# Two of twenty Strassen pieces as plain products, attention's values one item later, and earlier low parts before the first down product

## What is computed

```
# first block
x   = layer_norm(x)
o_a = rms_heads(fox_attention(q_a, k_a, v_a, logf))          # 8 heads of 64, causal, 4 query tiles each
o_r = rms_heads(hgrn2(q_r, k_r, i_r, logf_r)) * silu(g_r)    # recurrent heads
x   = layer_norm(alpha * x + concat(o_a, o_r) @ w_o)
h   = depthwise_conv(x @ w_up);  a, u = split(h)
x   = layer_norm(alpha * x + (gelu(a) * u) @ w_down)
# second block
x   = x + g1 * merge(neighbourhood_attention(...), hyena(...)) @ w_out
h2  = modulate(rmsnorm(x), sh2, sc2)
x   = x + g2 * (silu(h2 @ w1) * (h2 @ w3)) @ w2              # up: w1 and w3, down: w2
out = rmsnorm(x)
```

## Time and profile before

| | |
|---|---|
| three runs, us | 1707.61, 1707.92, 1709.17 (median 1707.92) |
| profiled execution, us | 1708.51 |
| its span, first to last instruction | 1706.7 |
| mean granted TensorE clock | 0.976 |
| busy: PE, DVE, ACT, POOL | 1595.5, 1056.9, 700.4, 439.5 us |

### The profile page before, as it was taken

How to read it: one execution, slowest core, us unless ns; L and a number is a source line. 1 busy time by engine, 2 the same in 40 slices (tenths; PEclk the granted TensorE clock), 3 DMA queues, 4 the chain that set the end, 5 groups by cost and what they waited for, 6 DMA issues and landing times. The chain is left out here.

```text
span 1706.7 us, 21205 instructions
## 1 busy us (share of the span) xinstructions
PE 1595.5 (93%) x8576; PEld 1335.1 (78%) x8576; DVE 1056.9 (62%) x1458; ACT 700.4 (41%) x1021; POOL 439.5 (26%) x360
## 2 busy tenths in 40 slices
PE   5999988988999999999799999998899899998996
PEld 5778875766878888788788778887787899998885
DVE  6675547447987486433765543346853699998333
ACT  5644245543533243323632334444444544443222
POOL 0023303320622011100052012223432655553002
PEclk8999999989999899999899999999999999999998
DMA  7242212342254254222426423224443132224211
GB/s 285 99 148 75 75 62 89 118 176 99 99 173 164 107 197 173 99 99 74 147 99 248 130 76 109 85 84 152 151 166 124 38 112 99 99 100 148 76 73 50
DMA packets 46924, 203.93 MB, mean 119 GB/s; under 512 B 14337, under 2 KB 14721, under 8 KB 28203
## 3 DMA queue, kind: packets, MB, share of 16 engines
q1 hardware_dynamic: 37202, 171.84, 28.1%
q0 software_dynamic: 9088, 30.38, 5.3%
q10 hardware_dynamic: 536, 0.35, 0.1%
HBM read 181.56 MB, written 21.00 MB: 119 GB/s over the span
## 5 line engine op out<-in xcount | busy, mean ns | idle before, releaser
L540 PE MATMUL ps<-xh,whi 128*128 128x512 f32 (+1 forms) x1096 | 395.5, 361 | 10.8 <-DVE wlo L1742 5.3
L542 PE MATMUL ps<-xh,wlo 128*128 128x512 f32 (+1 forms) x1096 | 390.0, 356 | 0.0
L541 PE MATMUL ps<-xl,whi 128*128 128x512 f32 (+1 forms) x1096 | 388.2, 354 | 0.0
L1742 DVE TENSOR_TENSOR wlo<-raw,whi 128x2048 fp32r<-128x2048 f32 x93 | 233.3, 2509 | 138.3 <-ACT whi L1132 138.3
L1132 ACT ACTIVATE whi<-raw 128x2048 fp32r<-128x2048 f32 (+1 forms) x173 | 221.9, 1310 | 137.8 <-PE ps L542 52.1
L540 PEld LDWEIGHTS ps<-xh,whi 128*128 128x128 f32 x1096 | 208.8, 190 | 53.0 <-issue 11.6
L541 PEld LDWEIGHTS ps<-xl,whi 128*128 128x128 f32 x1096 | 209.2, 191 | 29.3
L542 PEld LDWEIGHTS ps<-xh,wlo 128*128 128x128 f32 x1096 | 207.9, 190 | 31.0
L540 PE MATMUL ps<-whi,xh 128*128 128x512 f32 x304 | 122.9, 404 | 8.3 <-ACT vr L1132 3.7
L542 PE MATMUL ps<-whi,xl 128*128 128x512 f32 x304 | 121.8, 401 | 0.0
L541 PE MATMUL ps<-wlo,xh 128*128 128x512 f32 x304 | 121.6, 400 | 0.0
(11 more groups left out here) (449 smaller groups left out, 3358.2 us busy)
## 6 DMA issues: line engine op xcount, KB each, us to landing
raw<-in_w_in SPq DMA_DIRECT2D x35, 1024.0 KB, 5.1
raw<-in_ffn_w SPq DMA_DIRECT2D x33, 1024.0 KB, 4.8
raw<-in_ada SPq DMA_DIRECT2D x24, 1024.0 KB, 4.8
raw<-in_w_up SPq DMA_DIRECT2D x22, 1024.0 KB, 4.8
raw<-in_w_down SPq DMA_DIRECT2D x11, 1024.0 KB, 4.8
xd<-X POOLq DMA_DIRECT2D x8, 512.0 KB, 6.1
td<-vr POOLq DMA_DIRECT2D x16, 256.0 KB, 3.6
raw<-td SPq DMA_DIRECT2D x4, 1024.0 KB, 5.3
```

The lines of the kernel that those rows point to most:

```text
L540: pe.e.matmul(o, lh, rh, start=start, stop=False)
L541: pe.e.matmul(o, lh, rl, start=False, stop=False)
L542: return pe.e.matmul(o, ll, rh, start=False, stop=stop)
L1742: up(ve.e.tensor_tensor(lo, raw[conv_at[j] % 3][:, :], hi.bitcast(F32), ALU.subtract), "wlo")
```

## The change

**Attention.** The loop runs to 36; `gather` and DVE's `scaled` lag four items instead of three. The recurrent mixes come at items 11 to 14 instead of 9 to 12. After the loop `mix` 5 and 6 come ahead of the head norm 3, on DVE and on ACT; `last_mixed(3)` comes within the first group of rows of `w_o`, after two of its four tiles.

**First down product.** High and low parts of pieces 0, 1 and 2 are made at (j2, part) = (10, 1), ahead of the last two up tiles; `pieces` begins with 3.

**Last up product.** Pieces 0 and 19 (`SLOW`) are made by eight products (`whole_tile`: two tiles of 48 matmuls, each with two quarters of weights), with four low parts, no sums of weights and no sums of results. Weights have eight slots instead of ten, ACT leads by seven, DVE by six. The token sum of product 7 is kept in place (`xs7`), two strips of 128 columns a row. The first four buffers of the down operand move to ones that are free after n = 18, and J_DOWN2 is made high after n = 18 is done.

The diff, cut to its core:

```diff
+SLOW = (0, 19)
+FAST = [(n, p) for n in range(N_FAST) for p in ((11, 21, 12, 22) if n in SLOW else (1, 2, 5, 6, 3, 7, 4))]
...
+def slot(q):
+
+    return (q - len(FAST)) % 8
...
-        dn2 = [(flat(xh4[i // 2][0])[:, 512 * (i % 2):512 * (i % 2) + 512], flat(xl4[i // 2][0])[:, 512 * (i % 2):512 * (i % 2) + 512])
-               for i in range(4)]
+        dn2 = [(x[:, 0:512], x[:, 512:1024]) for x in (flat(s2h), flat(s2l), xrf[:, 3, :], flat(cl)[:, 1024:2048])]
...
-                    if 9 <= i <= 12:
-                        pe.wait_ge(sig["rec"], i - 8)
-                        mix_turn(i - 9, tiles_of(orr, i - 9))
+                    if 11 <= i <= 14:
+                        pe.wait_ge(sig["rec"], i - 10)
+                        mix_turn(i - 11, tiles_of(orr, i - 11))
...
-                if i >= 3:
-                    hd, t = divmod(i - 3, 4)
-                    gather(i - 3, pt1[(i - 3) % 3], [va[:, q, P * (hd // 2):P * (hd // 2) + P] for q in range(t + 1)])
+                if i >= 4:
+                    hd, t = divmod(i - 4, 4)
+                    gather(i - 4, pt1[(i - 4) % 3], [va[:, q, P * (hd // 2):P * (hd // 2) + P] for q in range(t + 1)])
...
-                    between=lambda: last_mixed(3))
+                    after=lambda n: None if n else last_mixed(3))
...
+            def whole_tile(n, m):
+
+                p1, p2 = ((11, 21), (12, 22))[m]
+                b = take(("fast", n, p2), *(("f_a", FA["gated" if m else "gated21", n]) if n % 2 else
+                                            ("f_s", FS[f"silu{p2}", n])))
+                pe.wait_ge(sig["wlo"], item_no(n, p2))
+                for c in range(2):
+                    for k in range(8):
+                        h, l = place(FAST_AT[n, p2 if k // 4 else p1])
+                        o = mm3(b[:, 256 * c:256 * c + 256], h[:, k % 4, :], l[:, k % 4, :], half_tokens(xh4, k, c),
+                                half_tokens(xl4, k, c), k == 0, k == 7)
+                done(o, ("fast", n, p2))
+                fills.at["fast", n, p1] = fills.n
...
             head_squares(7, oa, 3)
+            mix_high(5)
+            mix_high(6)
             spectrum(14)
             head_roots(ms_f[:, 24:32], 64, 8)
-            mix_high(5)
             spectrum(15)
-            mix_high(6)
             high(J_WO + 1)
...
+                    if (j2, part) == (10, 1):
+
+                        ac.wait_ge(sig["ch_lo"], 20)
+                        ac.wait_ge(sig["act"], 3)
+                        for k in range(3):
+                            act(dn1[k][0][:, :], act1[:, k, :], ACT.Copy, "sp_hi")
...
-                if q + 9 < len(FAST):
-                    fast_high(q + 9)
+                if q + 7 < len(FAST):
+                    fast_high(q + 7)
...
             for m in range(2):
                 b = tile(("u2", 0, 1, m))
                 ve.wait_ge(sig["f_s"], m + 1)
                 up(ve.e.tensor_tensor(act2[:, m, :], b[:, :], yg[:, 512 * m:512 * m + 512], ALU.mult), "f_a")
-            rows_sum(3, 7)
-            for q in range(5, 8):
+            for q in range(2, 6):
                 fast_low(q)
...
-                if q + 8 < len(FAST):
-                    fast_low(q + 8)
-                if q == 136:
+                if q + 6 < len(FAST):
+                    fast_low(q + 6)
+                if (n, p) == (N_FAST - 1, 21):
                     conv[0] = J_DOWN2
                     low_parts(J_DOWN2)
-                if q == 138:
-                    pieces(1, act2, dn2, only=range(4))
+                    for k in range(4):
+                        low_part(dn2[k][1], act2[:, k, :], dn2[k][0], "down1", k)
```

More of the change, by code:

```diff
@@ L212, with last_of, before @@
 for _n, _p in FAST:
-    for _x in (["s1"] if _p == 2 else []) + (["silu"] if _p == 1 and _n % 2 else []):
+    for _x in (["s1"] if _p == 2 else []) + (["silu"] if _p in (1, 11) and _n % 2 and _n - 1 not in SLOW else []) \
+            + ([f"silu{_p}"] if _p in (21, 22) and _n % 2 == 0 else []):
         FS[_x, _n] = len(FS) + 3
-    for _x in {5: ["c11"], 6: ["u2"], 7: ["u34", "c22"], 4: ["c"] + ["gated"] * (_n % 2)}.get(_p, []):
+    for _x in {5: ["c11"], 6: ["u2"], 7: ["u34", "c22"], 4: ["c"] + ["gated"] * (_n % 2),
+               21: ["gated21"] * (_n % 2), 22: ["gated"] * (_n % 2)}.get(_p, []):
         FA[_x, _n] = len(FA) + 3
-TS = {x: 17 + i for i, x in enumerate((n, p) for n in range(N_FAST) for p in (5, 7, 6, 4))}
+TS = {x: 17 + i for i, x in enumerate((n, p) for n in range(N_FAST) if n not in SLOW for p in (5, 7, 6, 4))}
+def slot(q):
+    return (q - len(FAST)) % 8
+def last_of(n):
+    return 22 if n in SLOW else 4
+def before(n):
+    while n - 1 in SLOW:
+        n -= 1
+    return n - 1
 def item_no(n, p):
@@ L463, in place @@
         def place(q):
[L465 to L472, removed]
+            s = slot(q)
+            b = buffer_of(J_DOWN2) if s < 4 else buffer_of(J_UP2 + 1)
+            c = 512 * (s % 4)
+            h, l = whi[b][:, c:c + 512], wlo[b][:, c:c + 512]
             return tuple(x.rearrange("p (k c) -> p k c", k=4) for x in (h, l))
@@ L805, in tensor_program @@
             use[0] = "attention"
-            for i in range(35):
+            for i in range(36):
                 if i < 32:
@@ L1423, in scalar_program, with pieces @@
                         channels(u)
-            def pieces(inst, src, dn, ready, first, begun=0, only=None):
+            def pieces(inst, src, dn, ready, first, begun=0):
                 def one(k):
@@ L1438, in one @@
                     act(dn[k % 4][0][:, :], src[:, k, :], ACT.Copy, "sp_hi")
-                for k in only or range(begun, 4):
+                for k in range(begun, 4):
                     one(k)
-                for k in range(0 if only else NFF):
+                for k in range(NFF):
                     if k % 2 == 0:
@@ L1683, in scalar_program @@
             fast_high(1)
+            ac.wait_ge(sig["ch_lo"], 37)
+            act(xs7[0], xs_src[7], ACT.Copy, "ch_hi")
             ac.wait_ge(sig["pe"], at["w", J_UP2])
@@ L1687, in scalar_program @@
                 b = tile(("u2", 0, 0, m))
-                ac.wait_ge(sig["ch_lo"], 39)
+                ac.wait_ge(sig["ch_lo"], 40)
                 act(yg[:, 512 * m:512 * m + 512], b[:, :], ACT.Silu, "f_s")
[L1690 to L1694, removed]
+            for q in range(2, 7):
                 fast_high(q)
             for q, (n, p) in enumerate(FAST):
-                if p == 1 and n % 2:
+                if p in (21, 22) and n % 2 == 0:
+                    b = tile(("fast", n, p))
+                    ac.wait_ge(sig["f_a"], FA["gated", n - 1] if n else 2)
+                    act(yg[:, 512 * (p - 21):512 * (p - 21) + 512], b[:, :], ACT.Silu, "f_s")
+                elif p in (1, 11) and n % 2 and n - 1 not in SLOW:
                     ac.wait_ge(sig["f_a"], FA["c", n - 1])
@@ L2155, in vector_program @@
                         ada_sums((12, 21).index(2 * j2 + part))
+                    if (j2, part) == (10, 1):
+                        for k in range(3):
+                            low_part(dn1[k][1][:, :], act1[:, k, :], dn1[k][0][:, :], "down0", k)
                     for m in range(2):
@@ L2167, in vector_program, with pieces @@
                         channels(u)
-            def pieces(inst, src, dn, begun=0, only=None):
+            def pieces(inst, src, dn, begun=0):
                 def one(k):
                     low_part(dn[k % 4][1][:, :], src[:, k, :], dn[k % 4][0][:, :], f"down{inst}", k)
-                for k in only or range(begun, 4):
+                for k in range(begun, 4):
                     one(k)
-                for k in range(0 if only else NFF):
+                for k in range(NFF):
                     if k % 2 == 0:
@@ L2439, in vector_program @@
             fast_low(1)
-            rows_sum(2, 3)
-            for q in range(2, 5):
-                fast_low(q)
+            ve.wait_ge(sig["ch_hi"], 39)
+            up(ve.e.tensor_tensor(xs7[1], xs_src[7], xs7[0].bitcast(F32), ALU.subtract), "ch_lo")
+            rows_sum(3, 3)
             for m in range(2):
```

110 lines of the change are left out of this document (60 added, 50 removed).

## The result

The changed kernel takes 1684.87 us (median of four, 1683.75 to 1690.43) against 1708.55 for the kernel before on the same chip: ratio 0.9865, 95% interval 0.984 to 0.9891, 23 us faster. The forecast was 1688.6 with a range of 1681 to 1700. The profiled run has a span of 1682.1 where before has 1706.7.

What follows compares the result with a forecast made beforehand. TensorE's work (93% of the span) plus its stops and half clock were taken as the bound. Gains of 6.6 (attention), 3.2 (first down product) and 9.5 (last up stage), 19.3 in all, took 1707.92 to 1688.6 us, range 1681 to 1700.

Steps and rivals of the forecast that it cites:

- Part A: Attention through the output product: fewer stops and less half clock, 6.6 us gained, bounds 2 and 12.
- Iterations 9 to 14: Attention loop: the 3.00 us stop on `pt`, half clock and smaller stops shrink; 4.0 us gained of at most 5.7.
- Iterations 30 to 35: End of the attention loop: two stops before `gather` and their half clock shrink; 2.0 us gained, 0.5 to 3.5 possible.
- Output product: Attention's end: `wo` starts 2.7 us earlier, `rows_last` only 2.3, less 1.7 of half clock; 0.6 us gained.
- Part B: First down product: early low parts let it start without its stop; 3.2 us gained, bounds 0 and 3.4.
- Part C: Last up stage: earlier start, fewer steady stops, earlier down product without half clock; 9.5 us gained, bounds 5 and 12.
- if DVE's cycle stays: Last up stage, steady part: DVE keeps 21.25 us a pair of pieces, so 4.8 us of 7.1 of stops remain.
- The first: Attention gives little, 0 to 2 us, as DVE or ACT bounds it and loads land late; 1694.2 us, chance 0.18.
- The second: Longer unbroken stretches of PE bring one more half-clock stretch without a stop; 1693.7 us, chance 0.10.
- The third: Last up stage: the shorter lead no longer hides late sums or copies, gain only 4 us; 1694.1 us, chance 0.12.
- the fourth: Last up stage: DVE's and PE's waits lock, pairs exceed 21.25 us; at 24.0 a pair 1710.6 us, chance 0.05.
- The fifth: Last up stage: first and last pieces keep their stops, no gain there, attention gives 1; 1703.7 us, chance 0.05.

Runs made afterwards that it cites:

- e1: The kernel before with the attention part of the change alone; ratio 0.9968, 5.5 us faster.
- e3: The kernel before with the last up product's part of the change alone; ratio 0.9911, 15.2 us faster.
- e4: The kernel before, ten slots and seven products in every piece kept, with ACT's lead cut from nine to seven and DVE's from eight to six; 0.9926, 12.7 us faster.
- e6: The changed kernel with DVE's lead seven instead of six; ratio to the kernel before 0.9906, 16.1 us faster than that.
- e5: The kernel before with DVE's lead seven instead of eight, ACT's left at nine; ratio 0.9967, 5.6 us faster.
- e9: The changed kernel unchanged, timed again on another chip as its measure; 1686.56 us, ratio to the kernel before 0.9876.

## Why the prediction was right, point by point

**Sum and sign.** 19.3 forecast, 23.1 measured (24.6 between the profiled runs). The sign, the places and the order of the parts were right; each part is told below.

**Part A, 6.6 forecast, 5.5 measured in e1.** The size came out right in part by luck: the terms didn't come as they were reasoned. Distances between the same matmuls of before and after give them. *Iterations 9 to 14, 4.0 forecast:* 3.5 from the matmul at 253.18 (252.06 in after) to item 20. The 3.00 us on `pt` went, as forecast. That nothing takes their place failed: the mix stands behind DVE's low part of `Xr` still, and that one takes 5.24 us now (it took 2.92 in the earlier trace rows). It ends 2.15 us behind GpSimd's second sum of the spectrum (288.67 to 289.96), and that of before ends 2.16 behind this one:

```profile
293.75 1.26 POOL L2508 TENSOR_TENSOR spo<-spe,spo 128x512 f32<-128x512 f32 x1
```

So of the 4.7 us that stop and clock could give, 0.5 came, and the half clock behind is as long as it was (3.4). The other 3.0 came from four shorter stops between 266 and 285, 3.75 together, which are one of 0.77 now and which the forecast had at about 1. *Iterations 30 to 35, 2.0 forecast:* 2.6 from item 20 to the end of PE's work ahead of `wo`. Its two stops stayed (1.28 and 2.24, were 1.60 and 1.70); one half-clock stretch less (1.7) and smaller waits made it. *Output product, 0.6 forecast:* 1.8 lost, the term of A that had the wrong sign. The step "wo starts with a stop of 1.2" failed: the stop is 4.46, on the PSUM bank that ACT's copy of spectrum 15 frees, with ACT's table load and root ahead of it. The clock there is 0.52 for 6.8 us, where the forecast had 1.00. I had followed that copy only to POOL and its loads, not to the bank. The step "row loads late, affine from 386.9" failed too: the loads are issued at 367.64 to 369.3 and land within 10.6 us, so by 380, and the affine operations start at 382.25 right behind the low part of 380.04, which hangs on ACT and that on PE's first half. So what was won ahead passed through, 5.9 us of it by 392.77, the stop there grew from 2.22 to 3.53, and half clock behind it took 1.7, as forecast. So 6.1 were won ahead of `wo`, where the forecast had 6.0 by other stops, and the output product gave some of it back instead of adding to it.

**Part B, 3.2 forecast, 3.3 in the traces.** Right in its steps: three low parts of 0.62 at 685.48, the convolution behind them not seen by PE, down without a gap.

**Part C, 9.5 forecast, 14.4 in the traces, 15.2 in e3.** Start: 2.1 forecast; n=1 starts at 1352.26 where it was 1364.79, less the 10.2 won before, 2.3. End: half clock behind the down start gone, 1.6. The term that was mis-sized is the steady part: "if DVE's cycle stays" 21.25, 4.8 us of stops remain. The cycle went to 20.15 and no stop remains: 4.8 us, the whole of the difference 14.4 − 9.5. So the sign "gates 21.25 apart" failed. I took DVE's 20.65 us in 21.20 as a load that the change can't touch; a third of it was contention: low parts cost 15.7 us a pair, 9.4 with GpSimd out of the way, 10.7 after. The lead of eight to six, which I priced as 2.9 us of lost slack, was, with ACT's from nine to seven, the main gain (e4: 12.7 of 15.2 us). That the gain of C was forecast at all rests on the start and the end; the steady part came larger than reasoned, and through a mechanism that the forecast doesn't have.

**Rivals.** The first (attention gives little) did not come: 5.5. The second, one more half-clock stretch without a stop, neither; the one at 572.8 is there again, and it is no evidence for that rival (see the last section). The third and the fourth were wrong in sign: the shorter lead made the pairs shorter. Pairs longer than 21.25 came only in e6, with one product of lead more than the change has, by slow low parts and DVE's waits for ACT. The fifth fell with e3.

## To carry to other kernels

When two elementwise engines work beside each other, an engine's busy share isn't a fixed load: look at the duration of one form of instruction alone and beside the other engine before taking its cycle as a bound. The distance of a software pipeline decides what lies beside what, so try it one up and one down; here one number was worth 5.6 us (e5), with ACT's lead beside it 12.7 (e4), and one product too many cost 5 to 7 (e6). When a stop's releaser is moved, follow every holder of what the waiting engine needs next, the PSUM bank too.

## What the hardware showed that I had not expected

DVE's subtraction of 128 x 512 takes 0.68 us alone and up to 1.77 beside GpSimd's sums; of 128 x 2048, 2.29 alone and 5.24 beside two of them. Of the 352 of 128 x 512 that start under a sum, 351 end 0.55 us behind the sum's end; the two of 128 x 2048 named above end 2.15 behind one. GpSimd pays too, less: one form of its sums (`raw<-raw,ts`) takes 1.29 us on average in after and 1.48 in before. DVE's sums from PSUM keep their 0.42 and 0.68.

The half clock with a busy TensorE is no accident of one run. It stands at the same place of the program in all fourteen traces of this case, 10.2 us long in eleven and 6.8 in three (e3, e4, e9). The profile calls TensorE busy there (10.00 of 10.00 us from 567.5 on in after), but the timeline says with what:

```profile
562.44 3.63 PE L640 MATMUL ps<-onesf,ch 128*128 128x1 f32 x32
565.92 5.94 PE L640 MATMUL ps<-onesf,cl 128*128 128x1 f32 x32
```

These are 64 matmuls of one column each, and the clock falls in the midst of them, at 567.1 in after and 572.8 in before, in each trace 4.2 to 5.3 us behind the first. Two groups of 20 such matmuls (at 676.9 and 947.7 in after) have no half clock at or right behind them in any trace. No run leaves the 64 out, so that they bring the fall isn't shown; but a busy share of 100% can be one column at a time, and the row at 572.8 in the earlier trace rows is no case of a clock that fell under full work. The Trainium skill, "TensorE: Matmul & The Clock Gate", section "What's actually happening", has activity release the throttle; whether matmuls of one column are such activity no run here tells, so the row doesn't speak against it, as the prediction had it.
